# A hybrid decoder step on one core: the single tokens' recurrence moved into the delta rule, with nine gates and 23 value rounds there, and the copies of their queries spread in two parts

## The reference, cut to what matters

```python
# mixer A, the 8 single tokens: 4 heads, an old state of 128 x 128 for each token and head
def step(state, xs):
    qt, kt, vt, gt, bt = xs
    state = state * jnp.exp(gt)[..., None, None]
    kv = jnp.einsum('bhd,bhde->bhe', kt, state)
    state = state + kt[..., :, None] * ((vt - kv) * bt[..., None])[..., None, :]
    return state, jnp.einsum('bhd,bhde->bhe', qt, state)
# then an RMS norm over each head's 128 outputs, times silu(z); the new state is an output too
# q, k, v come from a causal convolution over 4 rows (3 of them old), silu, and an L2 norm

# mixer B, the 8 single tokens: scores against all 2048 cached keys of 8 heads, the best 3 blocks
# of 256 by the mean key, a softmax over those and the own position, and the sum of their values
```

## Time and profile before

| what | value |
|---|---|
| median of three runs | 1119.39 us |
| the profiled execution, time / span | 1122.29 / 1120.5 us |
| PE busy | 1039.1 us, 93% |
| DVE / ACT / POOL busy | 568.9 / 384.8 / 180.3 us |
| mean granted clock of TensorE | 0.948 of full |
| moved by DMA | 152.68 MB, mean 136 GB/s |
| 103 to 135 us: PE busy | 17.37 of 32 us |
| 300 to 512 us: PE busy | 187.51 of 212 us |
| 512 to 642 us: PE busy | 114.10 of 130 us |

### The profile page before, as it was taken

The page is one execution under the profiler, slowest core; times in us unless marked ns, Lnnn a source line. Parts: engine busy times, 40 slices in busy tenths (PEclk is TensorE's granted clock), DMA queues, the critical chain, the costliest instruction groups (busy, mean ns, idle before and its releaser), DMA issues.

```text
span 1120.5 us, 20765 instructions
## 1 busy us (share of the span) xinstructions
PE 1039.1 (93%) x7990; PEld 962.1 (86%) x7990; DVE 568.9 (51%) x801; ACT 384.8 (34%) x630; POOL 180.3 (16%) x94
## 2 busy tenths in 40 slices
PE   6999599999779997996899999999999999999996
PEld 6999488888769876874586999999999999999996
DVE  5245588876999455343304265554334433434442
ACT  6443244454422232222100222344225314414532
POOL 0036855544565010000000000000000000000000
PEclk8999699999989998998857999999999999999999
DMA  8566766655454265667724154333322333332212
GB/s 253 147 227 182 236 204 191 178 160 152 131 162 141 58 179 150 192 196 221 202 75 132 52 175 123 106 95 95 94 86 88 92 95 94 94 94 85 85 54 76
DMA packets 179257, 152.68 MB, mean 136 GB/s; under 512 B 8913, under 2 KB 141723, under 8 KB 178918
## 3 DMA queue, kind: packets, MB, share of 16 engines
q1 hardware_dynamic: 163286, 137.58, 41.9%
q10 hardware_dynamic: 15896, 14.07, 4.2%
HBM read 142.78 MB, written 8.93 MB: 135 GB/s over the span
## 4 chain that ended last, share of the span: by engine, by line
PE 79%; DVE 10%; ACT 3%; POOL 3%; issue 2%; DMA 1%; SPq 1%; ACTq 1%; DVEq 0%; POOLq 0%
PE ps L445 58%; PE ps L1885 7%; PE ps L1876 3%; POOL ring L655 2%; DVE lg L1086 2%; DVE w_low L434 2%; PE ps L1755 2%; PE ps L1780 1%; PE ps L2003 1%; PE ps L1770 1%; PE ps L2019 1%; PE ps L1643 1%; PE ps L1604 1%; ACT w_high L429 1%; PE ps L1861 1%
## 5 line engine op out<-in xcount | busy, mean ns | idle before, releaser
L445 PE MATMUL ps<-xh,w_high 128*128 128x256 f32 x1216 | 265.3, 300 | 2.3 <-DVE An L1408 1.2
L445 PE MATMUL ps<-xl,w_high 128*128 128x256 f32 x1216 | 251.2, 289 | 0.0
L445 PE MATMUL ps<-xh,w_low 128*128 128x256 f32 x1216 | 250.6, 288 | 0.0
L434 DVE TENSOR_TENSOR w_low<-w_raw,w_high 128x1024 fp32r<-128x1024 f32 x125 | 159.7, 1278 | 152.9 <-ACT w_high L429 152.5
L429 ACT ACTIVATE w_high<-w_raw 128x1024 fp32r<-128x1024 f32 x125 | 132.3, 1058 | 289.4 <-PE ps L445 285.4
L445 PEld LDWEIGHTS ps<-xh,w_high 128*128 128x128 f32 x1216 | 194.8, 196 | 22.1 <-issue 19.7
L445 PEld LDWEIGHTS ps<-xl,w_high 128*128 128x128 f32 x1216 | 194.8, 194 | 0.0
L445 PEld LDWEIGHTS ps<-xh,w_low 128*128 128x128 f32 x1216 | 194.8, 194 | 0.0
L655 POOL TENSOR_TENSOR ring<-ring,qb 128x1024 f32<-128x1024 f32 x64 | 155.3, 2451 | 177.4 <-DMA qb<-qb_dram 75.0
L445 PE MATMUL ps<-mh,w_high 128*128 128x256 f32 (+1 forms) x640 | 128.6, 282 | 2.4 <-issue 2.4
L445 PE MATMUL ps<-mh,w_low 128*128 128x256 f32 (+1 forms) x640 | 128.9, 283 | 0.0
(11 more groups left out here) (365 smaller groups left out, 1287.6 us busy)
## 6 DMA issues: line engine op xcount, KB each, us to landing
ring<-in_cache_k SPq DMA_DIRECT2D x128, 256.0 KB, 3.0
ring<-in_cache_v SPq DMA_DIRECT2D x128, 256.0 KB, 3.0
w_raw<-in_w_in SPq DMA_DIRECT2D x66, 256.0 KB, 3.8
w_raw<-in_w_up SPq DMA_DIRECT2D x64, 256.0 KB, 3.0
w_raw<-in_w_down SPq DMA_DIRECT2D x64, 256.0 KB, 3.0
w_raw<-in_w_in ACTq DMA_DIRECT2D x24, 256.0 KB, 3.4
w_raw<-in_w_out SPq DMA_DIRECT2D x16, 256.0 KB, 3.1
ht_dram<-ht ACTq DMA_DIRECT2D x1, 2080.0 KB, 10.5
```

The lines of the kernel that those rows point to most:

```text
L434: dve.tensor_tensor(w_low[:, u % 2], w_raw[:, u % 4], w_high[:, u % 2].bitcast(F32), ALU.subtract).then_inc(S_lo, 1)
L445: last = pe.matmul(out[:, a:b], w[:, u % 2, k, :], x[:, i, a:b], start=(first + i == 0 and w is w_high and x is rhs_h), stop=(first + i == ...
```

## The change

**Keys and queries.** The spread of the queries is issued as two transfers, one for the first token and one for the other seven (`qb_landed`, `qb_rest`). DVE rotates them before it splits the weights of that iteration. PE turns a unit's result in the middle of the next unit's product, where it did so after it. Ten key pairs are handled in the units (two in each of 7 to 11, where it was three in each of 8 to 12), two per step in the attention's last eight steps, and 11 are left for the delta rule (13 before). POOL rotates the prompt's keys after 8 products and the new ones after 10 (6 and 9 before).

**The recurrence of the single tokens.** Its convolution, silu, squares and factors are done in attention steps 24 to 30. Products with the old state are taken for k and q together (`state_products`, 32 matmuls in all); the output is put together from these products, from the decay, and from the product of q and k (`new_outputs`), so the second pass over the new state goes away. For this the old state is loaded once more, by four transfers on ACT's queue between the attention and gate 0 (`sts`, `st`, `sts6`, `sts7`, 2 MB in all). The update of the state stays in the tail, its transfer at the same place.

**The tables.** Gate 8 and rounds 21 and 22 move into the delta rule, and the table puts gates, keys and rounds at other steps.

```diff
-    return 0 if u < 8 else 3
+    return 2 if 7 <= u < 12 else 0
 def keys_in_step(n):
-    return 2 if n % 8 == 5 else 1
...
 def delta_fill():
     fill = [[] for _ in range(len(delta_order()))]
     for i in range(GROUPS - KEYS_BEFORE):
-        fill[i].append(("key", i))
-    quarters = [0, 1, 2, 3, 5, 6, 7, 8, 10, 11, 12, 13, 15, 17, 18, 19, 21, 22, 23, 25, 33, 37, 41, 45, 52, 58, 64, 70]
+        fill[2 * i].append(("key", i))
+    quarters = [0, 0, 1, 1, 2, 2, 3, 3, 8, 9, 10, 11, 13, 15, 17, 19, 22, 25, 28, 31, 42, 43, 44, 45, 46, 47, 48, 50, 85, 87, 89, 90]
     for i, at in enumerate(quarters):
         fill[at].append(("gate", 4 + i))
-    steps = ("sel_turn", "sel_red", "sel2_turn", "select", "bias", "lg_bias", "lg_exp", "row_sums", "den", "den_out")
-    for name, at in zip(steps, (14, 15, 16, 17, 20, 21, 22, 23, 24, 25)):
+    for name, at in (("sm_prep", 2), ("sm_bcast", 4), ("sm_bc", 4), ("sm_delta", 9), ("sm_osq", 9), ("sm_osum", 10), ("sm_oms", 11),
+                     ("sel_turn", 24), ("sel_red", 25), ("sel2_turn", 26), ("select", 27), ("bias", 29), ("lg_bias", 30),
+                     ("lg_exp", 30), ("row_sums", 31), ("den", 32), ("den_out", 33), ("sm_oroot", 36), ("sm_on", 37),
+                     ("sm_oh", 40), ("sm_onl", 41)):
         fill[at].append((name, 0))
+    for b in range(NS):
+        fill[5 + b // 2].append(("sm_kv", b))
     for k in range(3):
-        fill[26 + 2 * k].append(("tail", k))
-        fill[27 + 2 * k].append(("tail_out", k))
+        fill[21 + k].append(("tail", k))
+        fill[22 + k].append(("tail_out", k))
     for r in range(ROUNDS_DELTA):
-        at = 28 + 3 * r
+        at = 33 + 13 * r // 5
         fill[at].append(("round", r))
         if r % 4 == 3:
...
-            sp.dma_start(qb[:].rearrange("p b c -> p (b c)"),
-                         bc(qb_dram.rearrange("(o b) c -> o (b c)", o=1), [P, NS * WB])).then_inc(qb_landed, 16)
+            for first, last, landed in ((0, 1, qb_landed), (1, NS, qb_rest)):
+                sp.dma_start(qb[:, first:last].rearrange("p b c -> p (b c)"),
+                             bc(qb_dram[first:last].rearrange("(o b) c -> o (b c)", o=1), [P, (last - first) * WB]))\
+                    .then_inc(landed, 16)
...
             for r in range(8):
-                if b * 8 + r == 6:
+                if b * 8 + r == 8:
+                    g.wait_ge(qb_rest, 16)
                     rotate_keys()
-                if b * 8 + r == 9:
+                if b * 8 + r == 10:
...
         attention_high(3)
+        act.wait_ge(S["pt_turned"], NA)
+        act.wait_ge(S["att_pv"], NA)
+        act.wait_ge(S["tm_turned"], NC12)
+        act.wait_ge(S["att_turned"], 4)
+        for dst, first, last in ((sts[:], 0, 4), (st[:], 4, 6), (sts6[:], 6, 7), (sts7[:], 7, 8)):
+            dst = dst.rearrange("p b h e -> p (b h) e") if last - first > 1 else dst
+            act.dma_start(dst, state_delta[0, first:last].rearrange("b h d e -> d (b h) e")).then_inc(st_landed, 16)
...
-                act.wait_ge(S["att_turned"], 4)
+            if n == 3:
+                act.wait_ge(*done("sm_kv"))
             A((gate_a if n < 8 else gate_b)[:, n % 8], gate_ps(n), ACT.Tanh, scale=0.5).then_inc(S["gate_out"], 1)
...
         n_red = 0
         for u, (kind, j, _) in enumerate(UNITS1[:U_C]):
...
             if u == 4:
                 v.wait_ge(S["mts_out"], 4)
                 sample_rotate().then_inc(*did("rope_q"))
...
+        def new_outputs():
+            v.wait_ge(*done("sm_kv"))
+            sums = bank(7, 192)[:, 128:192].rearrange("p (n w) -> p n w", w=2)
+            link(TT(dl[:], sums[:, :, 0], sbc[:, 0:32], ALU.mult))
+            link(TT(dl[:].rearrange("p (b h) -> p b h", h=HA), cvs[:, 8:12].rearrange(by_token),
+                    dl[:].rearrange("p (b h) -> p b h", h=HA), ALU.subtract))
+            link(TT(dl[:], dl[:], sbc[:, 32:64], ALU.mult))
+            link(TT(sn[:], sbc[:, 64:96], dl[:], ALU.mult))
+            link(TT(so[:], sums[:, :, 1], sbc[:, 0:32], ALU.mult))
+            TT(so[:], so[:], sn[:], ALU.add).then_inc(*did("sm_dlt"))
...
             pe.wait_ge(S_lo, u + 1)
             if u >= 2:
                 pe.wait_ge(unit_out, u - 1)
+            def between(k):
+                if k in (2, 6) and u <= 5:
+                    turn_raw(2 * u - 2 + k // 4)
+                if k == 4 and UNITS1[u - 1][0] in "qkv":
+                    turn_moba((u - 1) - (1 if u - 1 > 4 else 0))
+                if k == 6 and u == 11:
+                    sum_gates()
+                if k == 6 and u == 12:
+                    turn_moba_heads(5)
...
-            elif u <= 5:
-                product(pe, u, unit_ps(u % 2), xh, xl,
-                        before_k=lambda k: turn_raw(2 * u - 2 + k // 4) if k in (2, 6) else None)\
...
+        def spread_factors():
+            pe.wait_ge(S["att_norm"], 4)
+            mm(bank(7, 64), cf[0:NS, K_ONE:K_ONE + P], bd64[:], start=True, stop=True, skip_group_check=True)
+            pe.wait_ge(*done("sm_kq"))
+            mm(bank(7, 96)[:, 64:96], ones, so[:], start=True, stop=True, skip_group_check=True)\
+                .then_inc(*did("sm_bcast"))
+        def state_products(b):
+            if b == 0:
+                pe.wait_ge(*done("sm_bc"))
+                pe.wait_ge(st_landed, 64)
+            state_b = sts[:, b] if b < 4 else st[:, b - 4] if b < 6 else sts6 if b == 6 else sts7
+            for h in range(HA):
+                n = b * HA + h
+                last = mm(bank(7, 192)[:, 128 + 2 * n:130 + 2 * n], state_b[:, h], kq[:, n], start=True, stop=True,
+                          skip_group_check=True)
+            if b == NS - 1:
+                last.then_inc(*did("sm_kv"))
+        def sum_outputs():
+            pe.wait_ge(*done("sm_osq"))
+            mm(bank(7, 32), ones, sn[:], start=True, stop=True).then_inc(*did("sm_osum"))
         def turn_scores():
...
@@ -1982,57 +2089,35 @@
                     turn_values(k)
+        value_round(23)
         pe.wait_ge(S["on_gated"], NCH)
-        gate(8)
-        pe.wait_ge(*done("sm_sq"))
-        mm(bank(4, 64), ones, s1[:], start=True, stop=True).then_inc(*did("sm_sums"))
-        for n in (21, 22, 23):
-            value_round(n)
+        tr(bank(4, P, 32), dl[:], ident).then_inc(S["sm_t1"], 1)
+        tr(bank(5, P, 32), kq[:, :, 0], ident).then_inc(S["sm_t1"], 1)
         gate(9)
         value_round(24)
         turn_values(5)
-        pe.wait_ge(*done("sm_bd"))
-        mm(bank(5, 64), cf[0:NS, K_ONE:K_ONE + P], s1[0:NS, :], start=True, stop=True).then_inc(*did("sm_bsums"))
+        value_round(25)
         gate(10)
-        for n in (25, 26, 27):
-            value_round(n)
-        pe.wait_ge(*done("sm_decay"))
-        for b in range(NS):
-            for h in range(HA):
-                n = b * HA + h
-                last = mm(bank(4)[:, n:n + 1], state[:, n], s6[:, n:n + 1], start=True, stop=True,
-                          skip_group_check=True)
-            if b == NS - 1:
-                last.then_inc(*did("sm_kv"))
-            gate(11, b, b + 1)
-        pe.wait_ge(*done("sm_dlt"))
-        tr(bank(4, P, 32), s5[:], ident).then_inc(S["sm_t1"], 1)
-        tr(bank(5, P, 32), s6[:], ident).then_inc(S["sm_t1"], 1)
+        value_round(26)
+        value_round(27)
+        gate(11)
+        turn_values(6)
         value_round(28)
-        turn_values(6)
+        value_round(29)
         gate(12)
-        value_round(29)
+        value_round(30)
+        value_round(31)
         pe.wait_ge(*done("sm_bdo"))
+        pe.wait_ge(*done("sm_t1o"))
         for n in range(8):
             if n >= 2:
                 pe.wait_ge(S["sm_outer_out"], n - 1)
             mm(bank(4 + n % 2), knt[:], bd[:, 4 * n:4 * n + 4, :].rearrange("r n e -> r (n e)"), start=True, stop=True)\
                 .then_inc(S["sm_outer"], 1)
-        value_round(30)
-        gate(13)
-        value_round(31)
-        pe.wait_ge(S["sm_outer_out"], 8)
-        for b in range(NS):
-            for h in range(HA):
-                n = b * HA + h
-                last = mm(bank(4)[:, n:n + 1], state[:, n], cvs[:, h, b:b + 1], start=True, stop=True,
-                          skip_group_check=True)
-            if b == NS - 1:
-                last.then_inc(*did("sm_o"))
-            gate(14, b, b + 1)
-        turn_values(7)
-        pe.wait_ge(*done("sm_osq"))
-        mm(bank(5, 32), ones, s1[:, 0:32], start=True, stop=True).then_inc(*did("sm_osum"))
+            if n == 3:
+                turn_values(7)
+            gate(13, n, n + 1)
+        gate(14)
         gate(15)
```

236 lines of the change are left out of this document (136 added, 100 removed).

## The result

The changed kernel takes 1113.66 us (median of seven runs, 1111.02 to 1116.53), against 1121.75 us for seven runs of the kernel before: a ratio of 0.9936 with a 95% interval of 0.9912 to 0.996. So the change is worth 8 us, 0.6%, where 58 us were forecast, and the time lies 23 us above the range. The profiled execution has a span of 1111.7 us against 1120.5. A run more than 1.5% above the fastest of its kernel in its set counts as slow and is left out of the ratios, so a fast outlier of the kernel before shifts the ratio of its set.

The account below looks back on a forecast made before the run. PE was taken as bound by waits and lower clock in four places: 103 to 135, 300 to 345, 418 to 434 us and the tail. Terms -17 - 2 + 4 + 7 + 2 - 52 = -58 gave 1061 us, range 1041 to 1091.

Parts of the forecast that it names:

- A: Keys and queries, 103 to 135 us: earlier POOL start and five fewer products end DVE's waiting; -17 us, range -20 to -8.
- 61 to 64 us for 75.4: Front: POOL starts at 61 to 64 us instead of 75.4, needing only the first token and DVE rotating before its split.
- C: Attention's last eight steps: DVE's added reduces and small operations, nearer to hidden than not; +4 us, bounds 0 and +12.
- Nothing for it: Front: PE's turns in the middle of the next product were given no gain or loss.
- B: 135 to 145 us: ten busy us come at full clock if PE wasn't idle ahead; -2 us.
- D: Handover to the gates: gate 0's output on ACT stands behind state issues and held weights; +7 us, bounds +2 and +11.
- 14.4 us are free for 11.7: Attention's last eight steps: DVE has 14.4 us free for 11.7 us of added reduces and small operations.
- E: Delta rule: 16.4 us of added PE work, mostly covered by idle time and lower clock; +2 us, bounds -10 and +12.
- F: Tail: 129.3 us falls to 77, with 14 us of page waits and 3 for lower clock; -52 us.
- The pages: Rival: value pages bind from the first round on, the tail takes 105 us for 77, total 1089 us; chance 0.13.
- The front: Rival: POOL's chain of products stays last at 103 to 135 us, the gain there is -6, total 1072 us; chance 0.12.
- The clock: Rival: the lower clock stays behind the handover's idle time, making the kernel slower, up to 1248 us; chance 0.03.

Follow-up runs that it names:

- e15: Kernel before, with the change's key table for the units and the five remaining pairs taken in attention steps; 1113.72 us, ratio 0.9924.
- e9: Changed kernel with the front's old order (one queries' copy, old split, rotation and turn order), key table kept; 1097.1 us, ratio 0.9843.
- e13: Changed kernel with only PE's turns put back behind each unit; 1114.9 us, ratio 0.9951.
- e3: Changed kernel with one key pair instead of two in seven of attention's last eight steps, those seven pairs moved to the delta rule; 1106.43 us.
- e4: Changed kernel with the old state's four transfers issued behind gate 0 instead of ahead of it; 1111.32 us, ratio 0.9964.
- e6: Changed kernel with 28 of the 32 pairs of state products left out of the delta rule; 1109.71 us, ratio 0.9903.
- e1: Changed kernel with DVE's rotation of the prompt's queries one iteration earlier; 1113.91 us, ratio 0.9997.
- e2: Changed kernel with the new rows' six two-input products in attention replaced by products with a constant; 1115.79 us, ratio 1.0008.
- e11: e8 with the quarters of gates 2 and 3 moved beside the state products, in steps 5 to 12; 1098.2 us, ratio 0.9879.
- e8: Changed kernel with single keys in attention's end, state transfers behind gate 0, and DVE's query rotation and gate operations one iteration earlier; 1095.67 us, ratio 0.979.

## Why the prediction was wrong, point by point

**A, -17 forecast, -0.1 measured: the step that failed.** Its account of POOL and DVE in the kernel before was right in the main: with five products fewer in the units, and the old order, the wait of 17.0 us falls to 9.0 (e15) and 6.7 (e9), where none was forecast, and the first probabilities come at 123 us, an 11 us gain. It failed in "61 to 64 us for 75.4", and in taking an earlier POOL as good whatever it meets. POOL's first product came at 70.6 us, since the first token's copy, issued at 61.65 us with the larger one right behind, did not land before 70.2 (both issued within 1.62 us; that they shared the queues is likely and wasn't tried). And it met DVE's rotation, whose operations went from 0.42 to 2.45 us. I had a row for it, a split of 3.37 us beside 1.22, and set it beside C alone. "Nothing for it" on PE's turns in mid-unit was off by at most some 2.5 us (e13).

**B, -2 forecast.** It came about: the granted clock of the ten us behind the first probabilities is 1.00, with PE busy 10.00.

**C, +4 forecast, about +14.6 measured** (17.9 less D's 5.6, with B's -2.3 taken out). That is above the term's upper bound of +12. "14.4 us are free for 11.7" counted the small operations at 0.27 us each; the six beside POOL took 9.7 us together. Between the two marks DVE was busy 155.7 us for 134.2 before, 21.5 more and not 11.7: 9.2 for keys, 9.6 for the six products, the rest in other operations of the rows. e3 shows that the price of the six came with the doubled keys: 2.3 us with single ones.

**D, +7 forecast, +5.6 measured.** The size was right, the mechanism only in part: the time went into the issues of the state (5 us), while the weights behind them were held 1.42 us and not 7. e4 removes it.

**E, +2 forecast, +15.4 measured.** The work added on PE was put at 16.4 us, and its busy time grew from 187.5 to 211.0 us, 23.5: the products took 10.3 us for 7.6, partly at 1.2 GHz, and my mark for the stretch's end takes in one round more. The cover failed: idle time fell from 23.7 to 15.6 us, by 8.1, where 19.6 of idle time and clock was expected. The gap before 434 us did close (17.4 of 20 us busy from 420 to 440); the longest waits left are for DVE's `sqb` (3.1 us in two) and `bd` (2.6). e6 shows that the products themselves were on the path, for 5 to 10 us. Why the rest of the cover wasn't used stays open.

**F, -52 forecast, -43.0 measured.** PE's waits for pages in the tail are 7.0 us, not 14; the transfers reached 254 GB/s. What the term lacked was the clock. Busy time times what its clock misses to 1.00 gives an estimate of its cost: 42.80 x 0.14 + 22.84 x 0.28 for the two stretches above, and 13.4 x 0.15 for the last 13.6 us, 14.4 us in all, where 3 were put. The 79.0 us for which PE was busy, less these, are 64.6, so that its work was put 6 us too low as well, at 58.9. No experiment took the clock's part away.

**The rivals.** The pages did not bind: 1.8 us of waits in the whole delta rule. The front gave little, as one rival had it, but by another mechanism than POOL's own chain: DVE waited for POOL's products only 1.2 us up to 136 us. The clock stayed low for parts only, and made nothing slower than before. What none of the cases had is that two parts of one edit cancel. Their chances were set as if the terms' errors were independent; A and C had one cause, DVE's operations beside POOL, and went the same way.

## What to carry to other kernels

When an edit lets an engine start earlier, list what its neighbour does in the microseconds it now overlaps, and look up the same operation with and without that neighbour in the trace: one row at 1.22 us and one at 3.37 for the same split was the warning. Idle time counts as cover only where the engine that PE waits for has time as well; here DVE had none. And take a change of several parts apart before it is kept: here two lines of a table gave 8 us (e15), and the rest of the front took that back.

## What the runs showed of the hardware

Beside POOL's products (2.4 us each, both inputs in SBUF), DVE's operations on SBUF wait for up to one product each, however small: 2.33 us for 8x32 elements (L1270, 0.18 in e3), 2.32 for 128x20 (L1190 in e1, 0.18 in the changed kernel). It holds for one tensor with a constant as well (e2: 5.24 us for four against 5.41). A reduce did not wait: 1.20 to 1.22 us throughout. Nor did operations with one input in PSUM and one in SBUF: 0.68 to 0.69 us for `onb_l` and `att_n`, beside POOL at 181, 172 and 211 us.
The Trainium skill ("SBUF — State Buffer", "Who interferes with whom") has all three: two inputs in SBUF contend with a GpSimd instruction that reads SBUF, `tensor_scalar` can in its two-port mode, `tensor_reduce` never does. The traces agree with the first and the last; that the products with a constant waited fits the second, though no trace names their mode.

The granted clock was 0.50 from 345 to 350 us with PE busy 5.00 of 5.00, beside products of two columns, and 1.00 in the same stretch without them at 4.30 of 5.00 (e6). With a gate's matmuls between them it was 1.00 from 320 to 340 us, with PE busy 16.13 of 20, where it was 0.61 at 20.00 of 20 without (e11, e8). What it is about such products that goes with the lower clock, no run here tells.
